# DeltaNet solve: two semaphores for the returning inverse, a weight remainder computed later, a regrouped opening, and attention scores three blocks ahead

## The reference, cut to what matters

```python
# DeltaNet, 8 heads of 128, chunks of 64 tokens
lower = jnp.where(strict, jnp.einsum("bhncd,bhnkd->bhnck", k_beta, k) * decay, 0.0)
a_mat = lower + jnp.eye(CHUNK)
sol = lax.linalg.triangular_solve(a_mat, rhs, left_side=True, lower=True, unit_diagonal=True)
def step(state, xs):
    v_new = u_n - w_n @ state
    o = q_n @ state + a_n @ v_new
    state = state * jnp.exp(gl_n) + k_n.T @ v_new
# attention, 16 heads on 4 key heads, window of two chunks of 64
scores = jnp.einsum("bnqhgd,bnkhd->bnhgqk", q, kb) * (SW_HEAD_DIM ** -0.5)
probs = exp(scores - m) / (sum(exp(scores - m)) + exp(sink - m))
o = jnp.einsum("bnhgqk,bnkhd->bnqhgd", probs, vb)
```

## Time and profile before

| | us |
|---|---|
| median of 3 runs | 1419.47 (1418.46 to 1423.2) |
| the profiled execution | 1421.69 |
| its span in the trace | 1419.9 |
| TensorE busy | 1363.9 (96%) |
| VectorE busy | 794.3 (56%) |
| ScalarE busy | 533.0 (38%) |
| GpSimd busy | 252.2 (18%) |
| mean granted TensorE clock | 0.990 |

### The profile page before, as it was taken

The page is one execution under the profiler, slowest core; times in us unless marked ns, Lnnn a source line. Parts: engine busy times, 40 slices in busy tenths (PEclk is TensorE's granted clock), DMA queues, the critical chain, the costliest instruction groups (busy, mean ns, idle before and its releaser), DMA issues.

```text
span 1419.9 us, 18106 instructions
## 1 busy us (share of the span) xinstructions
PE 1363.9 (96%) x6594; PEld 1123.1 (79%) x6594; DVE 794.3 (56%) x1205; ACT 533.0 (38%) x901; POOL 252.2 (18%) x243
## 2 busy tenths in 40 slices
PE   7789999999899999999999999989999999999998
PEld 5678878888778888888888878758888888888877
DVE  5567777777574343343466677674443434435655
ACT  6444445444154132231334431453322313323344
POOL 3644555453030100000002110001010000000211
PEclk9999999999999999999999999899999999999999
DMA  6233233222323223223322352503322232223221
GB/s 178 62 84 78 57 83 84 55 61 69 99 75 118 90 90 118 89 89 104 103 89 86 93 100 64 119 1 104 116 93 89 89 115 93 89 89 100 85 83 60
DMA packets 168575, 125.67 MB, mean 89 GB/s; under 512 B 35873, under 2 KB 165186, under 8 KB 168514
## 3 DMA queue, kind: packets, MB, share of 16 engines
q1 hardware_dynamic: 167410, 123.01, 29.1%
q10 hardware_dynamic: 1104, 1.84, 0.5%
HBM read 116.96 MB, written 5.25 MB: 86 GB/s over the span
## 4 chain that ended last, share of the span: by engine, by line
PE 77%; DVE 11%; DMA 4%; ACT 3%; issue 2%; DVEq 2%; SPq 1%; POOL 0%; ACTq 0%; POOLq 0%
PE psum L148 21%; PE psum L150 21%; PE psum L149 21%; PE psum L890 2%; DMA xScaled<-inv_blocks 2%; DVE wL L140 2%; ACT wH L132 1%; PE psum L900 1%; PE psum L1917 1%; DVE terms L1166 1%; DMA inv_blocks<-blk 1%; DVE bL L1397 1%; DVEq L1168 1%; DVE hT L1598 1%; DVE acc L1596 1%
## 5 line engine op out<-in xcount | busy, mean ns | idle before, releaser
L148 PE MATMUL psum<-aH,wH 128*128 128x512 f32 x896 | 360.1, 402 | 12.2 <-issue 6.9
L150 PE MATMUL psum<-aL,wH 128*128 128x512 f32 x896 | 350.3, 391 | 0.0
L149 PE MATMUL psum<-aH,wL 128*128 128x512 f32 x896 | 349.6, 390 | 0.0
L140 DVE TENSOR_TENSOR wL<-wRaw,wH 128x2048 fp32r<-128x2048 f32 (+2 forms) x125 | 241.0, 1932 | 128.5 <-ACT wH L132 122.9
L148 PE MATMUL psum<-bH,wH 128*128 128x512 f32 x720 | 285.1, 396 | 2.3 <-DVE pleT L2043 1.6
L150 PE MATMUL psum<-bL,wH 128*128 128x512 f32 x720 | 281.0, 390 | 0.0
L149 PE MATMUL psum<-bH,wL 128*128 128x512 f32 x720 | 280.9, 390 | 0.0
L132 ACT CAST wH<-wRaw 128x2048 fp32r<-128x2048 f32 (+2 forms) x109 | 197.0, 1814 | 219.9 <-PE psum L150 219.9
L148 PEld LDWEIGHTS psum<-aH,wH 128*128 128x128 f32 x896 | 168.8, 188 | 45.6 <-issue 8.4
L150 PEld LDWEIGHTS psum<-aL,wH 128*128 128x128 f32 x896 | 168.5, 188 | 35.9
L149 PEld LDWEIGHTS psum<-aH,wL 128*128 128x128 f32 x896 | 169.0, 189 | 31.9 <-issue 0.5
(11 more groups left out here) (295 smaller groups left out, 1511.2 us busy)
## 6 DMA issues: line engine op xcount, KB each, us to landing
wRaw<-in_mlp_w_up SPq DMA_DIRECT2D x64, 512.0 KB
wRaw<-in_mlp_w_down SPq DMA_DIRECT2D x64, 512.0 KB
wRaw<-in_dn_w_in SPq DMA_DIRECT2D x32, 512.0 KB
wRaw<-in_ple_w_gate SPq DMA_DIRECT2D x16, 512.0 KB
xScaled<-inv_blocks SPq DMA_DIRECT2D x16, 256.0 KB, 3.1
wRaw<-in_sw_w_in SPq DMA_DIRECT2D x16, 256.0 KB
wRaw<-in_sw_w_out SPq DMA_DIRECT2D x16, 256.0 KB
wRaw<-in_dn_w_out SPq DMA_DIRECT2D x8, 384.0 KB
```

The source lines that it names most:

```text
L140: last = [nc.vector.tensor_tensor(o, r, h_.bitcast(F32), ALU.subtract) for o, r, h_ in zip(*([v if half is None else v[:, half * v.shape[1 ...
L148: nc.tensor.matmul(o, wh, xh, start=first, stop=False)
L149: nc.tensor.matmul(o, wl, xh, start=False, stop=False)
L150: return nc.tensor.matmul(o, wh, xl, start=False, stop=last)
```

## The change

Six things. (1) The inverse and its transpose get a semaphore each, on the way out and on the way back; SyncE reads the inverse back as soon as that one is written; `lower(0)` waits for the inverse alone and `corner(0)` for the transpose. (2) SyncE's `blocks_sp` is cut in two; the order of its work in the loop stays, but before the loop the first lower matrix goes ahead of the load of panel 4. (3) The second half of the remainder of the odd panel (`prep_lo(dve, n, 1, 1)`) leaves its place ahead of the block inverse: it goes behind `advance(2)` where there is a `p`, and behind `blocks_inverse(4)` where there is none. (4) Fills around it: two units fewer ahead of `walk(3)`, one more ahead of `update(3)` and one more behind it. (5) Opening: panel 2 is split before step a = 0, GpSimd sums the third tap before its decay matrices, and two units go ahead of the wait for the norms. (6) Attention's scores are issued three blocks ahead.

```diff
-        blk_out = sem("blk_out")
-        blk_in = sem("blk_in")
+        blk_out = [sem(f"blk_out{w}") for w in range(2)]
+        blk_in = [sem(f"blk_in{w}") for w in range(2)]
...
+        def blocks_sp(sp, a):
+
             sp.wait_ge(blk_ok, a + 1)
             for w in range(2):
-                sp.dma_start(...).then_inc(blk_out, 16)
-            sp.wait_ge(blk_out, 32 * a + 32)
+                sp.dma_start(...).then_inc(blk_out[w], 16)
             for w, dst in enumerate((inv, invT)):
-                sp.dma_start(dst, whole(invD.ap())[:, w]).then_inc(blk_in, 16)
+                sp.wait_ge(blk_out[w], 16 * a + 16)
+                sp.dma_start(dst, whole(invD.ap())[:, w]).then_inc(blk_in[w], 16)
...
-            for n in range(2, 5):
+            for n in range(2, 4):
                 load_panel(sp, n // 2, n % 2)
             sp.wait_ge(blank_out, 32)
+            lower_sp(sp, 0)
+            load_panel(sp, 2, 0)
             with sp.Fori(0, HEADS_A - 3) as a:
                 blocks_sp(sp, a)
                 load_panel(sp, a + 2, 1)
                 load_panel(sp, a + 3, 0)
+                lower_sp(sp, a + 1)
...
             def lower(i):
                 if i == 0:
-                    pe.wait_ge(blk_in, 32 * a + 32)
+                    pe.wait_ge(blk_in[0], 16 * a + 16)
...
                     pe.wait_ge(att_ok, a + 1)
+                    pe.wait_ge(blk_in[1], 16 * a + 16)
...
             if b is None:
                 gram_kk()
-            pe.wait_ge(ss_ok, 2 * a + 2)
-            solve(0)
-            if b is not None:
+                fill(2)
+                pe.wait_ge(ss_ok, 2 * a + 2)
+            else:
+                pe.wait_ge(ss_ok, 2 * a + 2)
+                solve(0)
                 gram_kk()
-            update(0)
-            fill(2)
+                update(0)
+                fill(2)
...
             update(2)
-            fill(4 if p is not None else 3)
+            fill(2 if p is not None else 3)
             walk(3)
             fill(2)
             solve(3)
-            fill(2 if p is not None else 1)
+            fill(3 if p is not None else 1)
             update(3)
             if p is not None:
-                fill(1)
+                fill(2)
...
# dn_step_act
-            if b is None:
-                prep_hi(act, n - 1, 0)
# dn_step_dve
-            if b is None:
-                prep_lo(dve, n - 1, 0)
...
             solved(1)
-            prep_lo(dve, n, 1, 1)
...
             blocks_inverse(4)
             if p is None:
+                prep_lo(dve, n, 1, 1)
                 out_early_dve(dve, 0)
             solved(2)
             blocks_inverse(8)
             blocks_out()
             advance(2)
+            if p is not None:
+                prep_lo(dve, n, 1, 1)
# dn_step_pool
-            if b is None:
-                taps_pool(pool, a, 2)
# dn_act
-            for b in range(2):
-                taps_act(act, 0, b, first=True)
-                tanh_act(act, 0, b)
+            taps_act(act, 0, 0, first=True)
+            tanh_act(act, 0, 0)
+            taps_act(act, 0, 1, first=True)
+            prep_hi(act, 2, 0)
+            tanh_act(act, 0, 1)
# dn_dve
-            for b in range(2):
-                silu_dve(dve, 0, b, 0, False)
+            silu_dve(dve, 0, 0, 0, False)
+            prep_lo(dve, 2, 0)
+            silu_dve(dve, 0, 1, 0, False)
# dn_pool
             taps_pool(pool, 0, 1)
+            taps_pool(pool, 0, 2)
# att_pe
-            scores(0, [1])
-            scores(1, [1])
+            for i in range(3):
+                scores(i, [1])
             keep_clock(8)
             for i in range(ATB):
                 t = i // KVH
-                if i + 2 < ATB:
-                    scores(i + 2, [1] if i < 2 else range(2))
+                if i + 3 < ATB:
+                    scores(i + 3, [1] if i < 1 else range(2))
```

More of the change, by code:

```diff
@@ L627, in diagonal, with lower_sp @@
             return d[:, :, 0:B16 * P].rearrange("w b (r c) -> b w r c", c=P)[:, :, :, 0:B16]
-        def blocks_sp(sp, a):
+        def lower_sp(sp, a):
             lo = lowD.ap().unsqueeze(0)
@@ L635, in blocks_sp @@
             sp.dma_start(lowBlk[0:NB, 0:B16 * B16].rearrange("b (r c) -> b r c", c=B16), diagonal(lo)[:, 0]).then_inc(low_in, 16)
+        def blocks_sp(sp, a):
             sp.wait_ge(blk_ok, a + 1)
             for w in range(2):
-                sp.dma_start(diagonal(invD.ap())[:, w], blk[0:NB, w, 0:B16 * B16].rearrange("b (r c) -> b r c", c=B16)).then_inc(blk_out, 16)
-            sp.wait_ge(blk_out, 32 * a + 32)
+                sp.dma_start(diagonal(invD.ap())[:, w], blk[0:NB, w, 0:B16 * B16].rearrange("b (r c) -> b r c", c=B16)).then_inc(blk_out[w], 16)
             for w, dst in enumerate((inv, invT)):
-                sp.dma_start(dst, whole(invD.ap())[:, w]).then_inc(blk_in, 16)
+                sp.wait_ge(blk_out[w], 16 * a + 16)
+                sp.dma_start(dst, whole(invD.ap())[:, w]).then_inc(blk_in[w], 16)
         def dn_sp(sp):
@@ L656, in dn_sp @@
             dn_out_load(sp, 0)
+            lower_sp(sp, HEADS_A - 2)
             blocks_sp(sp, HEADS_A - 2)
@@ L659, in dn_sp @@
             dn_out_load(sp, 2)
+            lower_sp(sp, HEADS_A - 1)
             blocks_sp(sp, HEADS_A - 1)
```

## The result

The changed kernel took 1432.13 us in the median of 7 runs (1426.78 to 1433.42), the kernel before 1419.47 in 7 runs beside it: a ratio of 1.0067, 95% interval 1.0044 to 1.0091. Slower: by 12.7 us in the medians, by 9.5 by the ratio. The profiled execution is the one of 1432.13 us, its span 1430.4, the mean granted clock 0.987 (before 0.990).

A forecast was written before the change was run, and what follows sets the result against it. TensorE, busy 96% of the span, was taken as the bound, so the change could only move its gaps. Opening 0.5 + loop 8.7 + clock 4.8 - step a = 7 0.3 - attention 0.9 = +12.8, 1432 us; range 1420 to 1438.

The forecast's parts named there:

- The fills and the moved remainder: Loop steps: gaps of 1.7 us at walk(3) and 1.3 at unit 16 delay lower(0) by 1.45; +8.7 us in six.
- The moved-away remainder gains nothing: Loop, ahead of the block inverse: VectorE waits longer for TensorE instead, blocks end as before; gain 0 (bounds 0 and 1.2).
- the forecast's sign: Loop steps of the changed kernel: VectorE's idle time at residual(2) would grow from 0.53 to above 0.9 us.
- The rival in which the inverse's chain moves up: Loop: blocks end 1.2 us earlier, -0.25 us a step, clock untouched; total 1412.8 us, faster than before; chance 0.07.
- The clock: TensorE in the loop: half clock behind the gaps costs 1.6 us in 3 of 6 steps; +4.8 us (0 to 9.6).
- all six steps would pay: Loop: the skill's clock rule alone would make every step lose clock; the forecast said the row at 84.37 contradicts it.
- The rival in which the clock holds: Loop: no 4.8 us clock loss, perhaps remainder not held; +8.0, down to +5, 1427.5 us (1424.5 to 1428); chance 0.24.
- The opening: Step a = 0: earlier copy of the lower matrix against unit 16 waiting some 8 us; +0.5 us (-4 to +3).
- Step a = 7: Last step: remainder ahead of solved(2) costs 0.9 us, split semaphore gains 1.2; -0.3 us (-0.9 to +0.9).
- Attention: Scores a block earlier remove VectorE's 0.43 us waits; net -0.9 us, about -5 if the clock fall goes, worst +0.5.
- The split semaphores: Loop: inverse back 0.4 to 1.0 us earlier, worth at most 1.10 us a step, nothing here as TensorE comes later.
- The sum: Whole kernel: the terms add to +12.8 us on the median of 1419.5, giving 1432 us.

The follow-up runs named there:

- experiment eleven: The changed kernel with 7 and 5 useless products filling TensorE's two gaps in each of the six loop steps: 1425.38 us, ratio 1.0055.
- experiment one: The changed kernel with the half remainder (also at a = 7) and the fills back in their old places: 1406.19 us, ratio 0.9903.
- experiment ten: The changed kernel run once more, nothing edited, on the same chip as experiment eleven: 1430.93 us, ratio 1.0082.
- experiment two: The changed kernel with only the half remainder back in its old place, a = 7 included, fills left as changed: 1414.17 us, ratio 0.9960.
- experiment three: The kernel before with the split semaphores alone: 1408.22 us, ratio 0.9922.
- experiment four: The kernel before with attention's scores issued one block further ahead, nothing else: 1418.68 us, ratio 0.9987.

## Why the prediction was right

1432.0 was forecast and 1432.1 measured, slower as expected. The gaps were where the forecast had them; that the totals agree to 0.1 us is luck, as the last paragraph shows. By its terms, in six steps and around them:

**The fills and the moved remainder: +8.7 forecast, +8.0 measured** (experiment eleven, 244.2 against 236.2). Both are net of what the split semaphores gain: beside experiment one's 228.3 the two edits cost 15.9. The working held in its parts: `walk(3)` idles 1.66 us (1.7), unit 16 then 1.10 (1.3), `lower(0)` waits for nothing. The remainder takes 1.61 us beside GpSimd's L802 and ends at 291.19, 1.09 behind it; I had said 1.2. The Trainium skill, "GPSIMD Engine Reference", section "Specifications", says in its row on SBUF interfaces that VectorE instructions with two SBUF inputs contend with GpSimd; the 1.61 against 1.21 agree.

**The moved-away remainder gains nothing: confirmed twice.** The idle time at `residual(2)` grew from 0.53 to 0.86 us, not above the 0.9 of the forecast's sign, and at `update(1)`'s state a new 0.59 appeared, while `blocks_out` stayed where it was (33.44 and 33.45). One unit taken from ahead of `walk(2)` on TensorE instead moved it by 1.45 us, 0.7 of them the unit itself. The rival in which the inverse's chain moves up is refuted.

**The clock: +4.8 forecast, 5.7 and 8.8 in two traces, 5.5 by the medians of ten and eleven and 3.8 by their ratios.** Mis-sized within its bounds: four steps of six and not three, and in two of them the clock stayed low for 2.8 us' worth and not 1.6. That all six steps would pay, the other case that the forecast names, came out in neither trace. The mechanism is shown: filled gaps, no falls. The rival in which the clock holds is refuted for this kernel; it held in experiment two, where only the first gap stood.

**The opening: +0.5 forecast, +1.0 and +0.8 in two traces.** Its steps came out within 0.8 us: the copy of the lower matrix at 62.26 (61.5, with bounds of 59.9 to 62.2), `blocks_out` at 76.26 to 76.6 (76.7), unit 16 idle for 8.68 (8), `lower(0)` at 88.95 (88.4). The +1.0 is a difference of two: the opening by itself gains 2.5 (85.41 in experiment one), and the moved remainder costs 3.5.

```profile
77.81 0.80 PE L148 MATMUL psum<-aH,wH 128*128 128x512 f32 x1 [8.68 <-DVE wL L140]
...
88.95 1.06 PE L898 MATMUL psum<-xScaled,work 128*128 128x128 f32 x8
```

**Step a = 7: -0.3 forecast, -0.7 measured.** The forecast's 0.9 - 1.2 took 1.2 for the split semaphores, which it had no row for and which does not go with its own 0.4 to 1.0 in the loop. Measured, the remainder costs 0.75 there (38.40 us for the step, 37.65 in experiment one) and the semaphores gain 1.5. One thing was missing: with the gap of 2.58 us down to 1.13 the fall behind it went too, about 1.6 us that the sum didn't have.

**Attention: -0.9 forecast, -0.5 for the new order.** VectorE's waits of 0.43 us for scores are gone, as forecast. The transposes' waits for probabilities did not shrink by them: 6.5 us at full clock under either order (experiment three and the changed kernel). The forecast's -0.9 is also not worked out of its parts. The trace shows -4.0, and without the other traces I would have put it down to the change.

**The split semaphores: 0.4 to 1.0 us a step forecast, at least 1.26 measured.** This is the step that the forecast had wrong, and it changed nothing in the sum, because the later `lower(0)` hid all of it. I had priced the first write's wait (0.53 measured, 0.43 said) and left the second read's landing nearly out. It mattered for the reading: the sum hides a part that gains 11 us by itself, and I had called 1.10 a step "the most".

**The sum.** The two profiled executions differ by 10.5 us in their spans: +1.0 in the opening, +16.8 in the six steps, -0.7 in the step to a = 7, -3.0 from there to attention (of which the missing fall explains 1.6; the rest is open), -4.0 in attention and +0.4 behind it. The loop's clock cost 4 us more than forecast in this trace, and attention and the stretch ahead of it 6 us less. The medians differ by 12.7 us, the ratio gives 9.5, and in experiment ten it is 13.9 and 11.6. So the forecast's +12.8 lies among these, and no closer agreement than 2 or 3 us can be claimed for it.

## What to carry to other kernels

Price each part as if it stood alone, too: here a part worth -11 us was hidden by two edits that cost 16 us in the six steps and the clock's share on top, and the sum alone would have thrown it away. Before moving work off an engine, ask who paces that engine: here the idle time ahead of its next two instructions said that nothing would come of it, and the other engine's order was the lever. A gap in a bound TensorE cost its length, a few tenths more for the stall, and at times the clock behind it; here two short gaps close together did what one long one did.

## What the runs showed of the hardware

Two gaps of 1.66 and 1.10 us, with 0.7 us of work between them, were followed by a granted clock of 0.50 in four of six steps, in two traces; a single one of 1.66 in none of six, a single one of 3.45 in five of six, and the single one of 2.58 at a = 7 in both traces that have it (the kernel before, experiment four). Useless products in the gaps took all falls away, in two traces of six steps.

Which engine gives way in the contention is not fixed: in these rows it is the one that started later, held until about the end of the other's instruction. In the loop VectorE's subtraction, started behind GpSimd's L802, was held: L802 ended at 290.10, 290.10 + 1.21 is 291.31, and the subtraction ended at 291.19, after 1.61 us instead of 1.21. In the opening it was GpSimd: its L755 took 3.15 us instead of 1.28 beside a subtraction that had started first and ended at 51.26; 51.26 + 1.28 is 52.54, and L755 ended at 52.39.

```profile
48.32 2.94 DVE L140 TENSOR_TENSOR wL<-wRaw,wH 128x2048 fp32r<-128x2048 f32 x1 [4.34 <-ACT wH L132]
```
```profile
49.24 3.15 POOL L755 TENSOR_TENSOR taps<-taps 128x510 f32<-128x510 f32 x1
```

In attention a fallen clock cost 0 to 6.6 us in kernels whose attention is the same; the spread of the runs of the kernel before (1414.3 to 1427.7 us) goes with its mean granted clock, 0.995 at 1414.3 and 0.984 at 1426.75.
